# One gate slot of the delta branch moved between the last attention heads of a hybrid mixer

## What is computed

```python
hcat = x @ w_in
qa, ka, va, qkv_b, beta_raw, dt_raw, z, gate_raw = jnp.split(hcat, SPLIT_POINTS, axis=-1)
ya = sliding_window_attention(qa, ka, va, pos_bias, sink)      # 16 heads
ya = ya.astype(x.dtype) @ w_branch_a
...
o = gated_delta_rule(qb, kb, vb, g, beta)                      # 8 heads
yb = o.reshape(b, l, V_B).astype(x.dtype) @ w_branch_b
gate_a, gate_b = jnp.split(jax.nn.sigmoid(gate_raw), 2, axis=-1)
return (gate_a * ya + gate_b * yb) @ w_out
```

## Time and profile before

| | us |
|---|---|
| median of 3 runs (2424.6 to 2425.63) | 2425.2 |
| the profiled execution, device time | 2425.95 |
| its span in the profile | 2424.2 |
| TensorE busy | 2279.1 (94% of the span) |
| VectorE busy | 1588.8 (66%) |
| ScalarE busy | 1140.6 (47%) |
| GpSimd busy | 371.9 (15%) |

### The profile page before, as it was taken

One profiled execution on the slowest core, in us unless ns is written; L12 is line 12 of the kernel. 1 busy time (PEld: TensorE's weight loads), 2 busy tenths in 40 slices (PEclk: granted clock), 3 DMA queues, 4 the chain that ended last, 5 costly groups with the idle time before them and its releaser, 6 DMA issues.

```text
span 2424.2 us, 37471 instructions
## 1 busy us (share of the span) xinstructions
PE 2279.1 (94%) x15862; PEld 2092.7 (86%) x15862; DVE 1588.8 (66%) x1858; ACT 1140.6 (47%) x1533; POOL 371.9 (15%) x305
## 2 busy tenths in 40 slices
PE   3879998888799999999999999999999999999998
PEld 3768887877799899998799889989999879988997
DVE  6988776499855754669755575465556985557545
ACT  2335344288444544456642454354345665235433
POOL 2112221211300210030033030012004003302100
PEclk9889999989899999999999999999999999999999
DMA  8868883434365465664431246546565453114652
GB/s 309 274 210 277 283 274 105 141 85 110 114 218 191 156 209 189 142 194 148 112 122 53 78 155 216 187 147 221 179 174 169 145 131 105 53 67 162 212 186 104
DMA packets 304282, 400.48 MB, mean 165 GB/s; under 512 B 43215, under 2 KB 262969, under 8 KB 304116
## 3 DMA queue, kind: packets, MB, share of 16 engines
q1 hardware_dynamic: 283360, 336.75, 43.4%
q0 software_dynamic: 17504, 57.89, 7.3%
q10 hardware_dynamic: 3252, 3.45, 0.4%
HBM read 393.86 MB, written 4.19 MB: 164 GB/s over the span
## 4 chain that ended last, share of the span: by engine, by line
PE 79%; DVE 14%; ACT 4%; issue 2%; DMA 1%; SPq 0%; DVEq 0%; ACTq 0%
PE tiles L496 16%; PE tiles L497 16%; PE tiles L498 16%; PE y_rows L496 6%; PE y_rows L497 6%; PE y_rows L498 6%; PE tiles L883 6%; DVE weights_lo L1367 2%; DVE ada_acc L1417 1%; ACT weights_hi L990 1%; DMA ada_ring<-in_ada_w_dram 1%; PE tiles L596 1%; DVE rnn_r L1688 1%; PE tiles L620 1%; DVE rnn_conv_out L1657 1%
## 5 line engine op out<-in xcount | busy, mean ns | idle before, releaser
L1367 DVE TENSOR_TENSOR weights_lo<-weights_raw,weights_hi 128x2048 fp32r<-128x2048 f32 (+2 forms) x316 | 768.1, 2437 | 509.1 <-ACT weights_hi L990 508.9
L496 PE MATMUL tiles<-xt_hi,weights_hi 128*128 128x256 f32 (+1 forms) x3216 | 919.1, 286 | 22.9 <-DVE weights_lo L1367 12.4
L497 PE MATMUL tiles<-xt_lo,weights_hi 128*128 128x256 f32 (+1 forms) x3216 | 912.4, 284 | 0.0
L498 PE MATMUL tiles<-xt_hi,weights_lo 128*128 128x256 f32 (+1 forms) x3216 | 912.3, 284 | 0.0
L990 ACT ACTIVATE weights_hi<-weights_raw 128x2048 fp32r<-128x2048 f32 (+2 forms) x316 | 593.0, 1880 | 210.2 <-PE y_rows L498 178.2
L496 PEld LDWEIGHTS tiles<-xt_hi,weights_hi 128*128 128x128 f32 (+1 forms) x3216 | 612.0, 190 | 39.9 <-issue 21.5
L497 PEld LDWEIGHTS tiles<-xt_lo,weights_hi 128*128 128x128 f32 (+1 forms) x3216 | 612.4, 190 | 2.8
L498 PEld LDWEIGHTS tiles<-xt_hi,weights_lo 128*128 128x128 f32 (+1 forms) x3216 | 612.0, 190 | 0.0
L496 PE MATMUL y_rows<-weights_hi,hid_hi 128*128 128x512 f32 x608 | 241.8, 398 | 0.0
L497 PE MATMUL y_rows<-weights_lo,hid_hi 128*128 128x512 f32 x608 | 239.3, 394 | 0.0
L498 PE MATMUL y_rows<-weights_hi,hid_lo 128*128 128x512 f32 x608 | 238.8, 393 | 0.0
(11 more groups left out here) (349 smaller groups left out, 3013.2 us busy)
## 6 DMA issues: line engine op xcount, KB each, us to landing
weights_raw<-in_ffn_w_dram SPq DMA_DIRECT2D x132, 1024.0 KB, 5.0
weights_raw<-in_mlp_w_dram SPq DMA_DIRECT2D x64, 1024.0 KB, 6.1
weights_raw<-in_w_in_dram SPq DMA_DIRECT2D x52, 1024.0 KB, 5.2
ada_ring<-in_ada_w_dram POOLq DMA_DIRECT2D x76, 512.0 KB, 4.9
weights_raw<-in_rnn_w_in_dram SPq DMA_DIRECT2D x16, 768.0 KB, 4.6
ada_ring<-in_ada_w_dram SPq DMA_DIRECT2D x20, 512.0 KB, 7.2
weights_raw<-in_w_in_dram SPq DMA_DIRECT2D x32, 256.0 KB, 4.3
weights_raw<-in_w_branch_a_dram SPq DMA_DIRECT2D x32, 256.0 KB, 4.8
```

What stands on the lines that cost most here:

```text
L496: pe.matmul(o, a, c, start=first, stop=False)
L497: pe.matmul(o, a, d, start=False, stop=False)
L498: return pe.matmul(o, b, c, start=False, stop=last)
L1367: dve.tensor_tensor(slot_view(WLO, m, NSPL), slot_view(RAW, m, NRAW), slot_view(WHI, m, NSPL).bitcast(F32), ALU.subtract).then_inc(*inc("l ...
```

## The change

In both mixers the slot gb 0 moves in the slot list from behind ba 3 to a place ahead of ba 0. PE runs it at j = 16, ahead of turn 14. DVE calls its `step` at j = 16, ahead of `norm_a(15)`. ACT calls its `step` and takes the sigmoid at j = 17, ahead of the copy of turn 15. Behind ba 3 only gb 1 is left ahead of the t0 groups. No work is added or removed, but for one more function table load on ACT in each mixer.

```diff
@@ plan
                         add_cols((s, "z", i), w, 4624 + 256 * i, 256)
+                    add_cols((s, "gb", 0), w, 6672, 256)
...
-                    for i in range(4):
+                    for i in range(1, 4):
                         add_cols((s, "gb", i), w, 6672 + 256 * i, 256)
@@ PE, mixer
                         cols_slot((s, "z", j - 12), XH, XL, "A")
+                    elif j == 16:
+                        cols_slot((s, "gb", 0), XH, XL, "A")
...
                 for hf in range(2):
-                    cols_slot((s, "gb", hf), XH, XL, "A")
+                    if hf:
+                        cols_slot((s, "gb", hf), XH, XL, "A")
@@ ACT, mixer
                         act.activation(TH[:, j % 2, :, :], pair_of(bank), ACT.Tanh, scale=0.5).then_inc(*inc("free_A", (s, "z", j - 12)))
+                    elif j == 17:
+                        gate("gb", 0)
...
-                for hf in range(2):
-                    gate("gb", hf)
+                gate("gb", 1)
@@ DVE, mixer
                         step((s, "z", j - 12))
+                    elif j == 16:
+                        step((s, "gb", 0))
...
                 for hf in range(2):
-                    step((s, "gb", hf))
+                    if hf:
+                        step((s, "gb", hf))
```

More of the change, by code:

```diff
@@ L1211, in mixer, with gate @@
                         act.activation(SEL[q:q + 8, :], IDN[q:q + 8, q:q + 8], ACT.Copy).then_inc(*inc("dn_tables"))
+                def gate(name, i):
+                    step((s, name, i))
+                    bank = tile((s, name, i))
+                    if name == "gb":
+                        evac((s, "gb", i), GBT[:, 2 * i:2 * i + 2, :], ACT.Sigmoid, pair_of(bank))
+                    else:
+                        if i:
+                            act.wait_ge(*past("gate_a_used", (s, i - 1)))
+                        evac((s, "ga", i), GT[:, :, :], ACT.Sigmoid, pair_of(bank))
                 for j in range(19):
```

## The result

The changed kernel takes 2444.04 us (median of 4 runs, 2443.74 to 2447.45), the kernel before 2425.41 beside it: a ratio of 1.0077, 95% interval 1.0064 to 1.0089. That is 18.6 us more, against 18.0 forecast (2443.2 us, range 2434.5 to 2449.0).

A forecast was written before the change was run, and what follows sets the result against it. TensorE was taken to bound the kernel (79% of the chain). Per mixer 10.3 - 5.8 + 2.4 + 1.5 + 0.8 = 9.2 us; 18.4 for both, less 0.4, gave 18.0 more: 2443.2 us, range 2434.5 to 2449.

The forecast's parts named there:

- slot ahead of turn 14: TensorE ahead of ba 0: with gb 0 in front, turn 14 starts at 1204.29, not 1199.69; +4.60 us.
- turn 14 to ba 0, clock up: Queues of ScalarE and VectorE delay turn 15, so ba 0 starts at 1215.15 after turn 14 at 1204.29; +5.70 us.
- slot gone behind ba 3: Behind ba 3: gb 0's time there falls away, -5.8 us, if what follows can come so much earlier.
- VectorE's list ahead of the levels, clock up: Between ba 3 and the levels: VectorE's list makes the level group late; +2.4 us, bounds 0 and 4.2.
- clock, turn 15 to ba 0: TensorE at the lower clock after 7.7 idle us, in both mixers; +1.5 us, bounds 0 and 2.4.
- clock around t0 and the first level group: TensorE may drop to the lower clock around t0 groups and levels; +0.8 us, bounds 0 and 1.7.
- the upper bound of 4.2: VectorE's list ahead of the levels: lateness if u0, split and u0 each waited for a GpSimd product.
- The clock stays up: Rival, 20%: TensorE's clock does not fall after the idle ahead of turn 15; 2438.6 us.
- The delta stretch hides DVE: Rival, 14%: GpSimd and VectorE miss each other ahead of the levels, 2.4 and 0.8 go; 2436.8 us.
- Faster: Rival, 5%: gb 0 fills TensorE's idle and nothing is late, 2.9 us a mixer gained; 2419.4 us.
- Everything meets: Rival, 7%: all terms of VectorE's list and clock at their upper bounds; 2450.4 us.
- No change: Rival, 4%: within 0.2%; the splits' order costs some 5 to 6 us in place of 10.3.

The follow-up runs named there:

- warm_long: Changed kernel with 63 identity transposes on TensorE ahead of turn 15, filling its idle: 2440.70 us, ratio 1.0053.
- dve_behind: Changed kernel with only VectorE's split of ba 1 moved behind norm_a(15): 2441.01 us, ratio 1.0052.
- act_early: Changed kernel with only ScalarE's split of ba 1 moved ahead of the exponentials of head 15: 2433.09 us, ratio 1.0029.
- both: Changed kernel with ScalarE's ba 1 split ahead of head 15's exponentials and gb 0's sigmoid behind the last output copy: 2430.38 us, ratio 1.0014.
- logs_early: Changed kernel with ScalarE's ba 1 split before head 15's exponentials, sigmoid behind last ot_hi, logarithms before turn 14's copy, VectorE's gb 3 split at first level: 2421.07 us.
- the missing control: The kernel before with its logarithms moved alone; not run, so no time.

## Why the prediction was right, step by step

The terms for one mixer, us, and what each measured; the clock is separated by warm_long, the rest read from the timelines. The mechanism came as forecast, queue by queue; the parts of the clock did not.

| term | forecast | measured |
|---|---|---|
| slot ahead of turn 14 | +4.60 | +4.43 |
| turn 14 to ba 0, clock up | +5.70 | +5.69 |
| slot gone behind ba 3 | -5.80 | -5.80 |
| VectorE's list ahead of the levels, clock up | +2.4 | +2.69 |
| clock, turn 15 to ba 0 | +1.5 | +1.03 |
| clock around t0 and the first level group | +0.8 | +1.64 and +1.12 (sublayers 5 and 8) |

*The slot.* Turn 14 came at 1204.91, 5.22 later, of which 0.79 lie ahead of the change (slot z 3 began at 1187.44, before at 1186.65). The sign in the prediction, "near 6 us later", was looser than its own 4.60.

*The queues.* The forecast of turn 14 to ba 0 was 1215.15 - 1204.29 = 10.86 us, and warm_long measured 10.85. The prediction's own pieces add to 1215.24 and not 1215.15 (1212.36 + 0.99 + 0.58 + 0.51 + 0.80), so the forecast was 10.95, and the agreement to 0.01 is chance. The idle ahead of turn 15 was 7.63 us for 7.7 and VectorE's 9.61 for 9 to 10; dve_behind, act_early and both took the path apart.

*The slot that is gone.* ba 0 to vt: 42.79 us before (1204.85 to 1247.64), 36.99 after.

*VectorE's list.* 13.33 us in warm_long less 10.64. The chosen half of a meeting with GpSimd was a whole one. Single instructions show how they meet, two of VectorE's, then one of GpSimd's:

```profile
1255.96 1.79 DVE L1823 TENSOR_TENSOR t_inv_t<-ident,l_level_t 128x512 f32<-128x512 f32 x1
1262.35 1.75 DVE L1823 TENSOR_TENSOR t_inv_t<-ident,l_level_t 128x512 f32<-128x512 f32 x1
```

```profile
1260.36 3.19 POOL L2057 TENSOR_TENSOR l_level_t<-la_decay,levels_t 128x512 f32<-128x512 f32 x1
```

Where none of the other kind is beside it, a u0 takes 0.68 us (a pair 1.28) and a product 1.28. The u0 at 1255.96 started beside a product that ended at 1257.20, and ended 0.55 behind it. The split started beside a product that ended at 1260.28, and ended 2.15 behind it (2.29 alone). The product at 1260.36 started beside the split, and ended 1.12 behind it, and the u0 at 1262.35 ended 0.55 behind that product. So each time the later one did nearly all its work after the earlier had ended. The Trainium skill's rule (SBUF — State Buffer, "SBUF: two separate sides"), that the one that starts first holds the shared ports for its whole length, agrees with these rows. What put the upper bound of 4.2 too high was the reading that u0, the split and u0 would each wait for a whole product: each waits only for what is left of the one under way.

*The clock* was right in its sum and wrong in its parts. Its first part, "I expect the lower level in both mixers", came true, but "what ba 0 loses beyond the 1.00 us of cover ... is 0 to 1.4" was nothing: 1.5 should have been 1.03. The part around the levels was 1.64 and 1.12 where I took 0.8. Together 2.67 and 2.15 us, against 2.3.

*What was missed.* The terms of sublayer 5 sum to 9.7 us. Those of sublayer 8, where turn 14 to ba 0 grew by 6.31 and vt to the levels by 3.62 and 0.2 more in the first level group, sum to 8.8, with 4.43 for its slot too (turn 14 is 13.63 later there, the scores behind z 3 9.20). With the 0.79 ahead of the change that is 19.2, and the span grew by 17.9. Some 1.3 us were given back behind the levels of sublayer 5, in a stretch where the granted clock had been 0.50 and is now 0.72, in the windows:

```profile
1386.45:1392.45 6.00, 5.70 (x36) 5.73 (x37) 5.36 (x9) 3.28 (x4) 0.52 (x1) 0.72 0.07 29
```

(0.72 - 0.50) x 6.0 = 1.3 us of full-speed time. No step of the prediction had this, nor the 0.79, and in part they cancel. The interval of the ratio is 15.5 to 21.6 us, so that 18.0 came within 0.6 of it is partly luck; what the traces bear out is 18.4 for the two mixers' terms.

*The rivals.* "The clock stays up", 2438.6, is what warm_long made true by force, 2440.7. "The delta stretch hides DVE" needed GpSimd and VectorE to miss each other, and they met. "Faster" named its point of decision rightly, that ScalarE's split of ba 1 be done before VectorE reaches it, but one condition was too few: act_early meets it and still is slower than before. It takes the sigmoid, the split of gb 3 and the logarithms too, and then 2421.07 stands near that rival's 2419.4. "Everything meets" had each term at its upper bound, and only the clock around the levels of sublayer 5 (1.64 of 1.7) came near it. "No change" needed the ba 1 split at its old relative time, and it came behind turn 14. The Trainium skill's advice to interleave stretches with different limits (Perfetto Trace Analysis, "Optimization Strategy") is borne out in logs_early, as far as the missing control allows, and not in the changed kernel, by what stood in the lists of the other engines.

## What to carry to other kernels

When a block moves on one engine, list what it brings onto the others' in-order lists and find for each item the next thing queued behind it: here a weight split for a later slot, needed by nobody for many us, stood between two heads, with a table load and a sigmoid behind it, and together they cost 5.7 us a mixer (10.85 in warm_long, 5.11 in the kernel both) where the moved slot could fill 2.9. Put such work where its engine idles for the moved block anyway, and anything not needed yet (a sigmoid, its table load) behind the last item that the bound engine waits for. And ask what the block had hidden at its old place: once it is gone, a list that was just short enough under it becomes the bound.

## What the runs showed of the hardware

- Transposes of 128 x 128 floats ran at 0.113 us each, 63 in 7.10 us. With 30 of them in the idle (4.21 us left) the granted clock still fell behind it; with 63 (0.61 left) it stayed at 1.00 through ba 0.
- A VectorE operation with two SBUF inputs and a GpSimd product that reads SBUF, started one inside the other, ran one behind the other: u0 1.79 and 1.75 us for 0.68, a split 2.96 for 2.29, a product 3.19 for 1.28. v_beta_rows, of the same shape and with a result tile and g_cols as inputs, took 1.28 us a pair beside a product, as a pair of u0 alone.
- Holding the clock up at turn 15 also took away the low stretch at the first level group some 50 us later, though the wait in front of it was the same (2.68 us for 2.67), and gave back the longer one further on. In warm_long's windows the stretch that had 0.72 in the changed kernel is at 0.50:

```profile
1388.90:1394.90 6.00, 5.75 (x27) 5.78 (x28) 5.33 (x10) 3.23 (x4) 0.57 (x2) 0.50 0.08 31
```

The profile of warm_long also runs 5.1 us later than the changed kernel's from ahead of the change on, so the trace doesn't say which of the two moved the stretches. And in the kernel called both, whose two mixers have the same lists, the first level group of sublayer 5 is at the lower level (behind a wait of 2.67 us) and that of sublayer 8 at the upper (2.53 us):

```profile
1259.87:1261.65 1.78, 1.78 (x10) 1.78 (x10) 0.00 (x0) 0.64 (x2) 0.00 (x0) 0.50 0.00 0
2057.04:2058.82 1.78, 1.78 (x18) 1.78 (x17) 0.00 (x0) 1.40 (x3) 0.65 (x2) 1.00 0.04 12
```

So a difference of 1 to 2 us between two kernels can be the place of a low stretch alone. Why nearly the same wait is followed by it in one case and not in the other, no run here settles.
- A table load on ScalarE took 1.28 us and the activation behind it started 0.01 to 0.02 us later (1210.61, 1211.91).
